# A one-core transformer block with a 32-expert layer: routing in groups behind the output projection, second biases as one product ahead of the experts

## What is computed

```python
x = x + mix @ w_out[l]
x = x + _moe(_rmsnorm(x, norm2_g[l]), w_router[l], b_router[l], w1[l], b1[l], w2[l], b2[l])
# _moe, per token t and each of its 4 experts e, with softmax weight w:
hh = t @ w1[e] + b1[e]                       # 2048 columns
glu = minimum(hh[:1024], 7); lin = clip(hh[1024:], -7, 7)
act = glu * sigmoid(1.702 * glu) * (lin + 1.0)
out[t] += w * (act @ w2[e] + b2[e])
```

## Time and profile before

| What | Value |
|---|---|
| median of 3 runs | 1612.62 us |
| the profiled execution's own time | 1610.17 us |
| its span in the profile | 1608.4 us |
| busy: PE, DVE, ACT, POOL | 1494.5, 1362.4, 1116.9, 141.4 us |
| granted PE clock, mean | 0.969 of full |
| attention with the input projection | 21.4 to 324 us |
| output projection's end and routing, to the first expert product | 324 to 398.24 us |
| experts, 32 items | 398.24 to 1587 us |
| moved by the DMA engines | 451.88 MB |

### The profile page before, as it was taken

How to read it: one execution, slowest core, us unless ns; L and a number is a source line. 1 busy time by engine, 2 the same in 40 slices (tenths; PEclk the granted TensorE clock), 3 DMA queues, 4 the chain that set the end, 5 groups by cost and what they waited for, 6 DMA issues and landing times.

```text
span 1608.4 us, 22317 instructions
## 1 busy us (share of the span) xinstructions
PE 1494.5 (93%) x7050; PEld 1196.9 (74%) x7050; DVE 1362.4 (85%) x1566; ACT 1116.9 (69%) x1305; POOL 141.4 (9%) x172
## 2 busy tenths in 40 slices
PE   6999998983899999999999999999999999999993
PEld 5777776763777777777777777777777777777772
DVE  5655556546899999999999999999999999999994
ACT  5455455251687778878777877787877787777874
POOL 5000000001000011001100000100010000011000
PEclk9999999995999999999999999999999999999997
DMA  8020210266799999999999999999999999999943
GB/s 249 1 79 15 65 53 30 86 231 249 271 349 367 361 354 360 360 354 351 354 358 359 359 360 360 356 354 365 343 359 350 353 362 362 357 360 358 346 160 120
DMA packets 100214, 451.88 MB, mean 281 GB/s; under 512 B 13504, under 2 KB 25792, under 8 KB 67408
## 3 DMA queue, kind: packets, MB, share of 16 engines
q1 hardware_dynamic: 90704, 434.55, 71.5%
q0 software_dynamic: 9472, 16.85, 5.1%
HBM read 445.05 MB, written 23.07 MB: 291 GB/s over the span
## 4 chain that ended last, share of the span: by engine, by line
PE 57%; DVE 25%; issue 12%; ACT 2%; DMA 2%; DVEq 1%; SPq 0%; POOL 0%; POOLq 0%; ACTq 0%
PE zpair L1717 39%; DVE stage_lo L934 13%; PE bank L1393 3%; PE bank L1395 3%; PE bank L1394 3%; DVE qk L1311 2%; DVE qk L1318 2%; DVE act_lo L1280 2%; PE bank L1693 2%; PE zpair L1467 1%; DVE qk L1307 1%; PE bank L1717 1%; PE bank L1531 1%; PE bank L1482 1%; PE zpair L1455 1%
## 5 line engine op out<-in xcount | busy, mean ns | idle before, releaser
L633 ACT CAST stage_hi<-ring 128x1024 fp32r<-128x1024 f32 x796 | 835.2, 1055 | 237.0 <-PE zpair L1717 170.7
L934 DVE TENSOR_TENSOR stage_lo<-ring,stage_hi 128x1024 fp32r<-128x1024 f32 x796 | 944.5, 1218 | 33.4 <-ACT stage_hi L633 10.4
L1717 PE MATMUL zpair<-stage_hi,act_hi 128*128 128x512 f32 x1024 | 327.2, 401 | 16.3 <-DVE stage_lo L934 14.3
L1717 PE MATMUL zpair<-stage_lo,act_hi 128*128 128x512 f32 x1024 | 317.5, 391 | 0.0
L1717 PE MATMUL zpair<-stage_hi,act_lo 128*128 128x512 f32 x1024 | 317.2, 391 | 0.0
L1717 PEld LDWEIGHTS zpair<-stage_hi,act_hi 128*128 128x128 f32 x1024 | 186.1, 189 | 74.1 <-DVE stage_lo L934 35.1
L1717 PEld LDWEIGHTS zpair<-stage_lo,act_hi 128*128 128x128 f32 x1024 | 193.3, 189 | 41.4
L1717 PEld LDWEIGHTS zpair<-stage_hi,act_lo 128*128 128x128 f32 x1024 | 193.1, 189 | 41.1
L1717 PE MATMUL bank<-stage_hi,act_hi 128*128 128x512 f32 x512 | 162.8, 399 | 0.1
L1717 PE MATMUL bank<-stage_lo,act_hi 128*128 128x512 f32 x512 | 159.4, 392 | 0.0
L1717 PE MATMUL bank<-stage_hi,act_lo 128*128 128x512 f32 x512 | 158.9, 391 | 0.0
(11 more groups left out here) (273 smaller groups left out, 1489.0 us busy)
## 6 DMA issues: line engine op xcount, KB each, us to landing
ring<-in_w SPq DMA_DIRECT2D x384, 1024.0 KB, 7.5
ring<-in_w_in SPq DMA_DIRECT2D x12, 1024.0 KB, 6.1
ring<-in_w_out SPq DMA_DIRECT2D x4, 1024.0 KB, 4.9
xs_all<-in_x SPq DMA_DIRECT2D x4, 512.0 KB, 7.5
ring<-in_x SPq DMA_DIRECT2D x4, 512.0 KB, 5.3
tn_scratch<-qk SPq DMA_DIRECT2D x4, 512.0 KB, 8.7
x_scratch<-ring SPq DMA_DIRECT2D x4, 512.0 KB, 9.5
ring<-x_scratch SPq DMA_DIRECT2D x4, 512.0 KB, 4.8
```

The lines of the kernel that those rows point to most:

```text
L633: nc.scalar.copy(dst, src).then_inc(split_hi, 1)
L934: nc.vector.tensor_tensor(dst, src, hi_ap.bitcast(F32), ALU.subtract).then_inc(split_lo, 1)
L1717: mm = pe.matmul(bank[b0 + h][:], w[:, k, :], m[:, j % STAGES, h * BANK:(h + 1) * BANK], start=False, stop=stop and w is T_lo)
```

## The change

- **Filler.** `streamed(q)` runs projection and stick-half output chunks as one stream over all 32 steps, six chunks ahead (`LEAD`). The forget logits come after tile 4, the forget gate's DVE and ACT work one step later (`F_STEP`). x2 is loaded in halves, the first two tiles when `split_lo` is 26.
- **First norm.** ACT takes Ln and Exp in place of Sqrt with DVE's reciprocal, from one table set loaded at the start; the transposes use eight banks.
- **Routing.** Token tiles are routed in the groups (0, 1), (2), (3): `lists`, `softmax`, `slots` on DVE, `positions` and `table` on PE, `payload` on POOL. The norm's product with g moves to POOL (`gained`), its scaling to ACT (`normal`). The table holds 32 items only; overflow items are worked out inside item 0 by `overflow`, `over_lists`, `over_tables` on DVE and 17 products and copies on POOL.
- **Second bias.** `bias_2` and `select2` are gone from all items. Instead the weights per token and expert (`dense`), transposed, are multiplied by all experts' b2 (`fold`, 8 products), copied out by ACT, and added to x2 by POOL (`fold_add`, 8 adds) before x2 goes to memory and before the first item's `bias_1`.
- **Gate.** ACT computes glu*sigmoid(1.702 glu) in one function; the DVE product L1318 is gone from all items.
- SP holds expert loads 6 and 7 until the first gather has landed, and the loads of the next item until the fold products are done and x2 is written.

```diff
+GROUPS = ((0, 1), (2,), (3,))
...
+LEAD = 6
+F_AT = 5
+F_STEP = 2
...
+def streamed(q):
+
+    return 0 if q < 0 else LEAD + (q + 1) * (FILLS + OUT_FILLS - LEAD) // (PARTS * STEPS)
+
+
 def filled(q):
 
-    return (q + 1) * FILLS // (PARTS * FILL_STEPS)
+    return min(FILLS, streamed(q))
 
 
 def finish(tile):
 
...
+    return next(q for q in range(PARTS * STEPS) if filled(q) >= KT * (tile - 2 + (tile >= F_AT)))
...
-            sp.wait_ge(split_lo, W_IN_PIECES + 4)
             for t in range(TT):
-                sp.dma_start(x2[t], x_d[t * P:(t + 1) * P, :]).then_inc(x2_in, 16)
+                if t % 2 == 0:
+                    sp.wait_ge(split_lo, W_IN_PIECES + 2 + t)
+                sp.dma_start(x2[t], x_d[t * P:(t + 1) * P, :]).then_inc(x2_in[t // 2], 16)
...
-                sp.dma_start(x2_d[t * P:(t + 1) * P, :], x2[t]).then_inc(x2_out, 16)
+            sp.wait_ge(oproj, 16)
+            for c in (4, 5):
+                load_w1(0, c, moe_slot(c))
             sp.wait_ge(logits_done, 1)
+            sp.wait_ge(gathered, 16)
...
-                    sp.wait_ge(tables, 1)
+                    sp.wait_ge(fold_mm, 2 * TT)
                 if c == 1:
-                    sp.wait_ge(bias_lo, 4)
+                    sp.wait_ge(bias_lo, 3)
                 if c == 2:
+                    for t in range(TT):
+                        sp.wait_ge(fold_added, 2 * t + 2)
+                        sp.dma_start(x2_d[t * P:(t + 1) * P, :], x2[t]).then_inc(x2_out, 16)
                     sp.wait_ge(x2_out, 16 * TT)
                     sp.wait_ge(x2_turned, 2 * TT)
-                if c == 4:
-                    sp.wait_ge(gathered, 16)
-                    sp.dma_start(gfb, norm_f_g.rearrange("(a d) -> a d", a=1).partition_broadcast(P)).then_inc(gf_in, 16)
                 load_body(1, 0, c, None if c < 4 else MAIN.freed_first(c - 4))
...
+            def gained(t):
+
+                pool.wait_ge(x2_add, 2 * TT + 2 * t + 2)
+                nc.gpsimd.tensor_tensor(tn[t], x2[t], g2b, ALU.mult).then_inc(x2_gained, 1)
+
+            def payload(g):
+
+                a, n = TOPK * GROUPS[g][0], TOPK * len(GROUPS[g])
+                pool.wait_ge(onehots, g + 1)
+                pool.wait_ge(w_ready, g + 1)
+                if g == 2:
+                    pool.wait_ge(tab_mm, 1)
+                for c, values in enumerate((row1, w_hi.bitcast(F32), w_lo)):
+                    ins = nc.gpsimd.tensor_tensor(pays[g][:, :, c, :], oh[:, a:a + n], values[:, a:a + n].unsqueeze(2).to_broadcast([P, n, E]), ALU.mult)
+                ins.then_inc(pay_ready, 1)
+
+            pool.wait_ge(g2_in, 16)
+            gained(0)
+            gained(1)
+            gained(2)
+            payload(0)
+            gained(3)
+            payload(1)
+            payload(2)
             pool.wait_ge(tn_out, 16 * TT)
-            pool.wait_ge(x2_out, 16 * TT)
             nc.gpsimd.memset(gath, 0.0).then_inc(gath_zero, 1)
             pool.sem_inc(yout_free, 1)
             pool.wait_ge(gath_zero, 1)
             pool.wait_ge(tables, 1)
-            for i in range(3):
...
+            def fold_add(n):
+
+                t, h = n // 2, n % 2
+                pool.wait_ge(fold_out, n + 1)
+                half = x2[t][:, h * BANK:(h + 1) * BANK]
+                nc.gpsimd.tensor_tensor(half, half, folded[n % 4], ALU.add).then_inc(fold_added, 1)
+
+            gather(0)
+            for n in range(4):
+                fold_add(n)
+            gather(1)
+            for n in range(4, 8):
+                fold_add(n)
...
+            step(nc.gpsimd.tensor_tensor(over_oba, oh, oba.unsqueeze(1).to_broadcast([P, 16, E]), ALU.mult))
+            summed(over_oba)
+            step(nc.gpsimd.tensor_tensor(oba_k, over_oba[:, :, 0], jm, ALU.add))
+            pool.sem_inc(over_item, 1)
+            pool.wait_ge(over_cmp, 1)
+            for c, values in enumerate((row1, w_hi.bitcast(F32), w_lo)):
+                nc.gpsimd.tensor_tensor(over_pay[:, :, c, :], over_hit, values.unsqueeze(2).to_broadcast([P, 16, WIDE]), ALU.mult)
+            summed(over_le)
+            nc.gpsimd.tensor_copy(eidx, over_le[:, :, 0]).then_inc(over_made, 1)
+            pool.wait_ge(x2_out, 16 * TT)
+            gather(2)
             with pool.Fori(2, E - 1) as i:
...
+                nc.scalar.activation(rs1[:, t:t + 1], ss1[:, t:t + 1], ACT.Ln, scale=1.0 / D, bias=epsc).then_inc(h_sq, 1)
+                act.wait_ge(h_sq, 2 * t + 2)
+                nc.scalar.activation(r1[:, t:t + 1], rs1[:, t:t + 1], ACT.Exp, scale=-0.5).then_inc(h_rs, 1)
...
+            nc.scalar.preload_act_table_set("gelu_apprx_sigmoid_and_others")
+
+            def fold_head():
+
+                act.wait_ge(tables, 1)
+                nc.scalar.copy(wtab[:, 0:E], bank[5][:, E:2 * E]).then_inc(wt_copied, 1)
+                act.wait_ge(dense_mm, 1)
+                nc.scalar.copy(wdT[0:96, :], bank[4][0:96, :]).then_inc(wdT_hi, 1)
+
+            def fold_evac(n):
+
+                act.wait_ge(fold_mm, n + 1)
+                if n == 0:
+                    act.wait_ge(tn_out, 16 * TT)
+                if n >= 4:
+                    act.wait_ge(fold_added, n - 3)
+                nc.scalar.copy(folded[n % 4], bank[n % 4]).then_inc(fold_out, 1)
 
...
-                nc.scalar.activation(sig, glu, ACT.Sigmoid, scale=ALPHA).then_inc(sig_done, 1)
+                nc.scalar.activation(sig, glu, ACT.Gelu_apprx_sigmoid).then_inc(sig_done, 1)
...
+                        if b == MOE0:
+                            fold_head()
+                            for m in range(4):
+                                fold_evac(m)
                         x_evac(q0)
+                        if b == MOE0:
+                            for m in range(4, 8):
...
+                        if j % 4 == 0:
+                            dve.wait_ge(x2_in[j // 4], 32)
...
+            def lists(g):
+
+                ts = GROUPS[g]
+                n = len(ts)
+                a = slice(TOPK * ts[0], TOPK * (ts[0] + n))
+                for t in ts:
+                    dve.wait_ge(lg_mm, t + 1)
+                    dve.wait_ge(r2_ready, t + 1)
+                    loose(nc.vector.scalar_tensor_tensor(out=lg[:, t * E:(t + 1) * E], in0=fbank[2 * t][:, 0:E],
+                                                         scalar=r2[:, t:t + 1], in1=brb, op0=ALU.mult, op1=ALU.add))
+                for t in ts:
+                    dve.wait_ge(steps["dve"], count["dve"] - n + 1)
+                    loose(nc.vector.max(v8[:, 8 * t:8 * t + 8], lg[:, t * E:(t + 1) * E]))
+                for t in ts:
+                    dve.wait_ge(steps["dve"], count["dve"] - n + 1)
+                    loose(nc.vector.max_index(i8[:, 8 * t:8 * t + 8], v8[:, 8 * t:8 * t + 8], lg[:, t * E:(t + 1) * E]))
+                v84 = v8.rearrange("p (t k) -> p t k", k=8)[:, ts[0]:ts[0] + n]
+                i84 = i8.rearrange("p (t k) -> p t k", k=8)[:, ts[0]:ts[0] + n, 0:TOPK]
+                nc.vector.tensor_tensor(w4[:, a].rearrange("p (t k) -> p t k", k=TOPK), v84[:, :, 0:TOPK],
+                                        v84[:, :, 0:1].to_broadcast([P, n, TOPK]), ALU.subtract).then_inc(exp_in, 1)
+                dve.wait_ge(steps["dve"], count["dve"])
+                chained(nc.vector.tensor_copy(kf[:, a].rearrange("p (t k) -> p t k", k=TOPK), i84))
+                chained(nc.vector.tensor_tensor(oh[:, a], iota_e.unsqueeze(1).to_broadcast([P, TOPK * n, E]),
+                                                kf[:, a].unsqueeze(2).to_broadcast([P, TOPK * n, E]), ALU.is_equal))
+                with nc.allow_low_precision(reason="the sum of at most one 1 and zeros is exact"):
+                    nc.vector.tensor_reduce(chosen[:, ts[0] * E:(ts[0] + n) * E].rearrange("p (t e) -> p t e", e=E),
+                                            oh[:, a].rearrange("p (t k) e -> p t e k", k=TOPK), AX.X, ALU.add).then_inc(onehots, 1)
+
+            def softmax(g):
+
...
+            for j in range(6):
...
+            add_oproj(1, 6, fbank[6])
+            lists(0)
+            add_oproj(1, 7, fbank[7])
+            softmax(0)
+            lists(1)
+            slots(0)
+            softmax(1)
+            lists(2)
+            slots(1)
+            softmax(2)
+            slots(2)
+            dve.wait_ge(counted, 1)
+            nc.vector.tensor_copy(cnt, bank[1][:, 2 * E:3 * E]).then_inc(cnt_copied, 1)
+            dve.wait_ge(tab_mm, 3)
+            nc.vector.tensor_scalar(gtab[:, 0:E], bank[5][:, 0:E], AWAY, None, ALU.add).then_inc(tables, 1)
+
+            chained(nc.vector.tensor_tensor(dense_k, oh, w4.unsqueeze(2).to_broadcast([P, 16, E]), ALU.mult))
+            for r in range(3):
+                ins = nc.vector.tensor_reduce(dense[:, :, r, :], dense_k.rearrange("p (t k) e -> p t e k", k=TOPK), AX.X, ALU.add)
+            ins.then_inc(dense_r, 1)
+            dve.wait_ge(bias_hi, 2)
```

(53 more changed lines are left out.)

541 lines of the change are left out of this document (288 added, 253 removed).

## The result

The changed kernel takes 1566.42 us (median of 4 runs, 1565.0 to 1567.0) against 1612.72 for the kernel before on the same chip: a ratio of 0.972, 95% interval 0.970 to 0.974. That is 46 us less where 63 to 65 were forecast: the direction holds, and the time is 18 us above the 1548 of the prediction and inside its range (1524 to 1575).

A forecast was written before the change was run, and what follows sets the result against it. Attention was taken as PE-bound with stalls, routing as a line of DVE work, the expert loop as PE-bound with a DVE chain. Terms summed to -62.7, from 1610.2 to 1547.5, named 1548; range 1524 to 1575.

The forecast's parts named there:

- Filler ahead: Attention: k tiles finished a step sooner end PE's stalls and half clock, -20; new wait at tile 4's bank, +3.
- x2 in halves: Attention, fox cycle with the x2 loads: first half there three steps ahead removes most of the 8.5 us excess, -6.5.
- Routing: Last add to x2 to first expert product: routing in groups brings tables and first product earlier, -20.7.
- about 350: Time in us at which the first expert product was expected, against 398.24 before.
- Item 0: First expert item: overflow work on DVE and POOL lengthens it and the way to item 1, +9.5.
- Loop: Expert loop: gate product's removal ends a 0.82 us wait, second bias buys nothing; item 35.9, 31 bodies -25.4.
- Tail: Behind the last item: L1318 and the second bias both stand on the path, -1.6.
- DMA: Rival, expert loop: DMA can't go faster, item stays at 36.73, 1573 us; chance 0.10.
- table loads: Rival "slower", expert loop: ACT's new gate function adds two table loads of 1.28 us per item, 1630; chance 0.04.
- Both chains loosening: Rival: POOL's hits miss PE in item 0 (-8), loop gives 1.1 an item (-9), 1531 us; chance 0.16.
- attention or item 0 give half: Rival: stalls return at the next late producer (+10) or POOL is slow (+10), 1558 to 1568; chance 0.15.

The follow-up runs named there:

- e4: Changed kernel with the filler shared out over the attention steps as before (no chunks ahead, forget gate's projection first), x2 still in halves: 1580.5 us.
- e5: Changed kernel with the four x2 loads issued together again instead of in halves: 1566.7 us.
- e8: Changed kernel with 41 extra PE products of 128 rows and 512 columns in the routing, their result overwritten: 1565.7 us.
- e6: Changed kernel without the work that finds the overflow items' lists (POOL products and adds, DVE compares and small instructions, PE's second table): 1559.0 us.
- e7: Changed kernel with the fold's eight adds to x2 on DVE, straight from the banks, instead of ACT copies and POOL adds: 1559.65 us.
- e2: Changed kernel with two extra PE products per item where the second bias stood, their result overwritten: 1565.6 us, item 36.03.
- e3: Changed kernel with the low part of the next item's turned tokens one w2 piece later in DVE's order: 1558.75 us, item 35.80.
- e11: Changed kernel plus fold adds on DVE, next item's low part later, early x2 add, overflow tables among item 1's first pieces, filler four chunks ahead: 1548.2 us.
- e1: Changed kernel with one extra DVE instruction of 128x1024 per item where the first gate product stood: 1581.3 us, item 36.52.

## Why the prediction was right, and where it was too good

**Filler ahead (-20 and +3): right in kind, the +3 too small.** e4 puts both together at 14.1 us by the times, 12.6 to 15.6 by the marks (290.55 against the 275.0 to 278.0 of the executions with the filler ahead), where 17 was forecast. The mechanism (k tiles a step sooner, no stand, no half clock) is shown by the window of 94 us without a pause and by e4's stands. The new wait at tile 4's bank was named at its place, 2.70 where 2 was taken. What the prediction did not have is a second one: the stand at the add to x2, 4.22 against 0.70 in e4. It and the stands for `pt_lo`, which stood in the kernel before (1.38, 1.39 and 1.83) and which the prediction does not name, are what was left. One reading was also short: the stand at 65 us is 2.57 long (it ends at 66.66), of which the window of the earlier trace rows, opened inside it, holds 1.65.

**x2 in halves (-6.5): wrong.** This is the term that failed. The record took the fox cycle's whole excess of 8.5 us for the loads', since DVE's stand of 5.86 lay in it. e5 gives the edit at most 1 us of PE's idle time and no time that can be measured, and e4 shows 37.85 of the 38.39 with x2 on time. The cycle's idle time of PE, 38.39 - 32.54 = 5.85, is the sum of the three stands shown above: 1.83 for `pt_lo`, 2.79 for the output projection's stage piece, 1.23 behind `v_lo`. None is for x2. The normal cycle has 1.38 of idle time, so 4.5 of the excess are these and 4.0 are busy time, mostly the half clock behind them. DVE's stand began behind the last of these stands and PE waited 0.51 us for what followed. A stand on an engine is a cost only where the bound engine then waits, and no row said it did.

**Routing (-20.7, measured -16.3).** From the tables on the working held: 8.05 us to the first fold product (8 in the record), and 9.3 to the first expert product instead of 8.5, since POOL's adds at 1.24 us and more hold back ACT's copies. The other 3.5 us are in front of the tables. Rows of the changed kernel, the last one a window from the end of the last add to x2 to the tables:

```profile
333.59 0.62 POOL L667 TENSOR_TENSOR pay<-qk,cols 128x256 fp32r<-128x256 f32 x1 [8.29 <-DVE qk L1384]
...
335.31 2.41 POOL L657 TENSOR_TENSOR qk<-ring 128x1024 f32<-128x1024 f32 x1
...
336.72 2.07 DVE L1397 TENSOR_TENSOR ohslot<-iotas,qk 128x1024 fp32r<-128x1024 f32 x1
...
337.75 1.15 ACT L955 ACTIVATE qk<-qk,cols 128x1024 f32<-128x1024 f32 x1 [2.08 <-POOL qk L657]
...
339.03 0.16 DVE L1380 TENSOR_REDUCE qk<-qk 128x1 f32<-128x4 f32 x1 [0.23 <-ACT qk L961]
```
```profile
332.57:347.06 14.49, 9.82 (x61) 9.10 (x60) 11.57 (x43) 9.96 (x15) 7.25 (x11) 0.60 0.55 207
```

The prediction took 8.6 us from the last tile's logits to the tables, and let DVE start on them as soon as they were there: at 352 on the time scale of the kernel before, 38.5 us behind the mark of the fox output projection. What it had wrong is this start. The logits end 42.7 behind the mark (338.68), and by its own order DVE is not free before 43.9. Behind the last add to x2 it first has the softmax of the first group, the lists of tile 2, the slots of the first group and the softmax of tile 2, 7.3 us, 6.35 of them busy; it takes up the last tile's lists at 339.89. From there to the tables it is 7.2 us, less than the 8.6. There is a chain over other engines in the rows (DVE's softmax of tile 2 waits for an exponential on ACT, which stands behind ACT's norm of tile 3, which waits for POOL's product, which stands behind three payload products), but DVE waits for it only 0.23 us. More is in the 2.07 us that one DVE instruction takes beside POOL's product: the same line takes 0.70 at half the columns, so some 0.7 us by this estimate. The record priced POOL's product at 2 us with an upper end of 2.85; the four take 2.39 to 3.44. (The Trainium skill, GPSIMD Engine Reference, section 3.1, gives 4497 ns for an add of 2048 elements; the estimate of 2.2 from it is nearer to the rows than the value taken, and also below them.) That the clock is not in it is shown: in e8 and e4 the last logits ran at full clock and end 1.4 us sooner behind the mark, and the routing takes 68.3 and 68.4 as well. That DVE's order is the cause is read from the rows; no run changed it.

The line "about 350" of the record is also a slip: 398.24 less 24.5 and 20.7 is 353. Measured 364.4, the sum of what attention and routing left out.

**Item 0 (+9.5, measured +8.0, in which an item of the loop with its -0.7 is counted).** The right kind and nearly the size, for a partly different reason, so the nearness is in part luck: the lists cost 6.8 (e6), and the largest single hit is not on POOL but on DVE (5.62 us) by the fold's adds; taking these away gives 5.8 (e7).

**Loop (-0.82 an item, measured -0.66 to -0.70).** The claim that bias 2 buys nothing is shown by e2 for this order of DVE (e2 and e3 together leave 0.23 for it in another), and the short wait at the seventh piece is there. The size was off because 0.82 is the wait of the weight load, while PE itself stood 0.40 in the same place; what the gate product gave is 0.70 (36.73 to e2's 36.03), between the two. The short wait that came at the seventh piece (0.22 on PE, 0.65 on the weight load) costs 0.26 and lay one call away (e3).

**Tail (-1.6, measured +0.6).** L1318 does not stand on the path there: PE's w2 of the item before ends at the same distance behind the clip. Bias 2 does, and its 0.5 us went (from the clip to the end of the last output copy 31.13 before, 30.59 now, at the same mean clock of 0.94). From there to the end it took 1.1 us more, 23.4 for 22.3. That part lies between 22.2 and 23.4 in all the executions here, so it says nothing of the change.

**The rivals.** DMA and table loads are excluded by rows above. Both chains loosening (1531) did not happen either, though e11's 1548 shows that half of the distance to it was there to be had. The time fell where "attention or item 0 give half" had put it (1558 to 1568, chance 0.15). In part that is its reason too: a stand came back at a late producer, the add to x2. The larger part is another: a term in attention that was nothing, DVE's own work ahead of the last lists in the routing, and 0.16 us too much in each of 31 items. Nearly all misses were to the same side, and the range held since it had been made wide for rivals that did not come.

## What to carry to other kernels

Give an excess to the engine that bounds the stretch: list the bound engine's own stands in it first, and a stand of another engine only with the row in which the bound engine then waits for it. Of a wait shown on the weight load and on the product, take the two as ends (0.82 and 0.40 here, and 0.70 measured), and price it with the next limit behind it. When a rest is priced from the moment its input is there, look where the engine that does it stands in its own order at that moment. When work is moved to an idle engine, write down what stands behind it in order on that engine and on those that wait for it; and try a waiting call one position later before anything larger.

## What was not expected of the hardware

One DVE instruction of 16 columns took 5.62 us (0.17 without) beside four POOL adds of 512 columns: the exclusion holds DVE off too, for several POOL instructions in a row. The Trainium skill, SBUF — State Buffer, section Who interferes with whom, names both directions; the trace now agrees for both, and e7 shows that without the adds the instruction is short.

The same attention code took 275.0 to 278.0 us by the marks in seven executions (the changed kernel, e1, e2, e3, e6, e7, e8). PE's idle time was the same, 15.2 us, in the shortest and in one of the longer ones; what differed is where the clock fell. The first row is the whole stretch in e3. The other two are the 7 us from 260 on, behind the same stand of PE: first the changed kernel (stand of 2.75 at 258.68), then e3 (2.74 at 258.20).

```profile
21.01:313.25 292.24, 277.00 (x1492) 223.22 (x1493) 174.01 (x274) 141.91 (x243) 3.94 (x3) 0.98 0.20 62
```
```profile
260.00:267.00 7.00, 6.96 (x41) 5.27 (x39) 3.49 (x8) 3.58 (x7) 0.00 (x0) 1.00 0.36 143
```
```profile
260.00:267.00 7.00, 7.00 (x30) 5.36 (x29) 1.29 (x6) 0.95 (x5) 0.00 (x0) 0.55 0.30 119
```

PE stood just as long in both, and only in one did the clock fall. e3 has 2.5 us more busy time than the changed kernel's profiled execution for the same products. Differences under 3 us in such a stretch are to be read from idle time, not from its length.
